# Staging of queries and keys split into four half buffers, with new scratch layouts in HBM

## The reference

```python
h = rmsnorm(x, norm1_g)
p = einsum('bsd,de->bse', h, w_in)          # u, then dq, dk, dv (4 heads x 2 x 64), then sq, sk, sv (4 heads x 64)
a_out = pool_mixer(u, pool_w, pool_scale)
b_out = diff_attention(dq, dk, dv, ...)     # softmax(q1 k1) - lam * softmax(q2 k2), causal, times v
c_out = stick_breaking_attention(sq, sk, sv, ...)
x = x + concat(a_out, b_out, c_out) @ w_out
x = x + (silu(rmsnorm(x) @ w_gate) * (rmsnorm(x) @ w_up)) @ w_down
return rmsnorm(x, final_norm_g)
```

## Time and profile before

| | us |
|---|---|
| median of 3 runs | 3868.71 (3867.44 to 3869.24) |
| the profiled execution | 3868.71 |
| its span, first to last instruction | 3867.0 |
| TensorE busy in it | 3738.0 |

### The profile page before, as it was taken

The page is one execution under the profiler, slowest core; times in us unless marked ns, Lnnn a source line. Parts: engine busy times, 40 slices in busy tenths (PEclk is TensorE's granted clock), DMA queues, the critical chain, the costliest instruction groups (busy, mean ns, idle before and its releaser), DMA issues.

```text
span 3867.0 us, 58782 instructions
## 1 busy us (share of the span) xinstructions
PE 3738.0 (97%) x24256; PEld 3121.5 (81%) x24256; DVE 1735.1 (45%) x3306; ACT 1424.1 (37%) x2568; POOL 485.5 (13%) x243
## 2 busy tenths in 40 slices
PE   8989999999999989899999999999999999999999
PEld 7878778978887878777788887788888777887887
DVE  5757624551644353444555444454445443122113
ACT  4322431331232343465555555444445541021001
POOL 2102130000000000233333301100000100000000
PEclk9999999999999999999999999999999999999999
DMA  8746677557655867666675754555554434564544
GB/s 307 263 164 232 231 265 258 200 207 252 217 192 191 290 201 259 213 222 235 230 248 206 242 202 146 170 170 169 166 166 169 156 131 161 195 235 163 196 185 163
DMA packets 198874, 799.34 MB, mean 207 GB/s; under 512 B 20816, under 2 KB 70224, under 8 KB 130384
## 3 DMA queue, kind: packets, MB, share of 16 engines
q1 hardware_dynamic: 198608, 795.59, 59.1%
HBM read 594.18 MB, written 201.33 MB: 206 GB/s over the span
## 4 chain that ended last, share of the span: by engine, by line
PE 89%; DVE 3%; ACT 3%; DMA 3%; issue 1%; POOL 0%; SPq 0%; DVEq 0%; ACTq 0%
PE bank L1365 85%; PE bank L1369 4%; DVE P L2433 1%; SPq L2625 0%; DMA zraw<-in_x_t_dram 0%; DMA R<-X1d 0%; POOL slot L2587 0%; DVE R L2104 0%; DMA Y2d<-PY 0%; DVE Z1a L2150 0%; ACT L1899 0%; DMA slot<-Wd 0%; ACT Z1a L1756 0%; DMA R<-in_x_n_dram 0%; ACT L1968 0%
## 5 line engine op out<-in xcount | busy, mean ns | idle before, releaser
L1365 PE MATMUL bank<-Z1a,slot 128*128 128x512 f32 x3048 | 782.1, 401 | 9.5 <-DVE slot L2045 9.5
L1365 PE MATMUL bank<-Z1b,slot 128*128 128x512 f32 x3048 | 782.6, 401 | 2.5 <-DVE Z1b L2150 2.5
L1365 PE MATMUL bank<-slot,Z0b 128*128 128x512 f32 (+1 forms) x3504 | 712.8, 354 | 9.9 <-DVE R L2104 8.8
L1365 PEld LDWEIGHTS bank<-Z1a,slot 128*128 128x128 f32 x3048 | 564.2, 189 | 139.8 <-DVE slot L2045 9.5
L1365 PEld LDWEIGHTS bank<-Z1b,slot 128*128 128x128 f32 x3048 | 566.3, 189 | 137.1 <-issue 7.0
L1365 PEld LDWEIGHTS bank<-slot,Z0b 128*128 128x128 f32 x3504 | 562.6, 189 | 104.3 <-DVE R L2104 11.6
L2587 POOL TENSOR_TENSOR slot<-raw,slot 128x1024 fp32r<-128x1024 f32 x117 | 292.1, 2503 | 688.9 <-ACT slot L1783 688.5
L2104 DVE TENSOR_TENSOR R<-R,bank 128x512 f32<-128x512 f32 x352 | 239.0, 686 | 244.6 <-PE bank L1365 244.3
L2599 POOL TENSOR_TENSOR Z0b<-AF,Z0b 128x512 fp32r<-128x512 f32 x88 | 142.0, 1614 | 1290.6 <-ACT Z0b L1975 1290.6
L2401 DVE TENSOR_SCALAR_CACHE_REDUCE P<-bank 128x512 f32<-128x512 f32 (+3 forms) x320 | 188.0, 609 | 255.1 <-PE bank L1365 254.2
L1365 PE MATMUL bank<-KS,DQ 128*128 128x512 f32 (+3 forms) x960 | 275.3, 388 | 21.6 <-DVE P L2401 9.4
(11 more groups left out here) (230 smaller groups left out, 4352.5 us busy)
## 6 DMA issues: line engine op xcount, KB each, us to landing
slot<-Wd SPq DMA_DIRECT2D x390, 1024.0 KB, 5.0
Wd<-slot SPq DMA_DIRECT2D x130, 1024.0 KB, 7.5
raw<-in_wts_dram SPq DMA_DIRECT2D x130, 512.0 KB, 4.3
DQ<-Qd SPq DMA_DIRECT2D x192, 128.0 KB, 3.7
DV<-Vd SPq DMA_DIRECT2D x60, 256.0 KB, 4.5
Kd<-QS SPq DMA_DIRECT2D x24, 512.0 KB, 5.1
Qd<-QS SPq DMA_DIRECT2D x24, 512.0 KB, 6.6
KS<-Kd SPq DMA_DIRECT2D x24, 512.0 KB, 7.1
```

What stands on the lines that cost most here:

```text
L1365: return e.matmul(o, a, b, start=start, stop=stop, skip_group_check=True)
```

## The change

`QS` becomes four buffers of 512 numbers per partition in the same space: two for high parts (0 and 2), two for low parts (1 and 3). High and low parts are stored by a transfer of their own each (256 KB): the high part waits for ScalarE only, the low part for VectorE. ScalarE now waits for the landing of the high part of two results ago, and for VectorE's reading of it; VectorE waits for the landing of the low part of two results ago. `Kd` becomes [head pair, high/low, partition, token], `Qd` becomes [head pair, 64, head of the pair, high/low, token], and `DQ` becomes [partition, 4, token]. The planner is not touched: the orders of TensorE, VectorE, ScalarE and GpSimd stay the same, and SyncE's gets 48 more issues (1298 rows where 1250 were).

```diff
-                  two("QS", [128, 2 * SUB]) + two("PT", [128, 16 + SUB]))
+                  two("QS", [128, SUB], F32, 4) + two("PT", [128, 16 + SUB]))
...
-        Kd = dram("Kd", [6, 128, 2, T])
-        Qd = dram("Qd", [6, T // 128, 128, 2, 128])
+        Kd = dram("Kd", [6, 2, 128, T])
+        Qd = dram("Qd", [6, 64, 2, 2, T])
...
-                mm(b[:, 0:w], DQ[:, qt, 2 * r, :], ks[:, at:at + w], True, False)
+                mm(b[:, 0:w], DQ[:, 2 * r, tok(qt)], ks[:, at:at + w], True, False)
...
-                i = m % 2
+                i = 2 * (m % 2)
                 if m >= 2:
                     act.wait_ge(*d_qs[i](*qkv_of[m - 2]))
                     if is_v(qkv_of[m - 2][2]):
                         act.wait_ge(*d_qv[i](*qkv_of[m - 2]))
+                    else:
+                        act.wait_ge(*dve_g("ev", ("C",) + qkv_of[m - 2][1:3]))
+                to = QS[i][:, :] if is_v(n) else QS[i][:, :].bitcast(F32R)
+                e.activation(to, b[:, :], ACT.Copy).then_inc(*act_g.inc("ev", label))
...
+                d = d_qs[i + 1]
+                if (k := qkv_of[m]) in d.at and d.at[k] > d.whole:
+                    dve.wait_ge(d.sem, d.at[k] - d.whole)
+                e.tensor_tensor(QS[i + 1][:, :].bitcast(F32R), b[:, :], QS[i][:, :], ALU.subtract).then_inc(
                     *dve_g.inc("ev", label))
...
-                sp.wait_ge(*dve_g("ev", ("C", s, n)))
-                if n % 2:
-                    to = Qd[x, NT * s:NT * s + NT].rearrange("c p a t -> p c (a t)")
-                    transfer(to, QS[i][:, :].rearrange("p (c n) -> p c n", c=NT), d_qs[i], *label)
-                else:
-                    to = Kd[x, :, :, SUB * s:SUB * s + SUB]
-                    transfer(to, QS[i][:, :].rearrange("p (a t) -> p a t", a=2), d_qs[i], *label)
+                t = slice(SUB * s, SUB * s + SUB)
+                for part in range(2):
+                    sp.wait_ge(*(dve_g if part else act_g)("ev", ("C", s, n)))
+                    to = Qd[x, :, :, part, t].rearrange("p h t -> h p t") if n % 2 else Kd[x, part, :, t]
+                    transfer(to, QS[i + part][:, :], d_qs[i + part], *label)
...
+                    at = SUB * s + 128 * x
                     for rep in range(2):
-                        to = DQ[64 * rep:64 * rep + 64, x, :, :].bitcast(F32).rearrange("p (h a) t -> p h (a t)", h=2)
-                        transfer(to, Qd[e_, NT * s + x].rearrange("(h p) a t -> p h (a t)", h=2), d_dq[x],
+                        to = DQ[64 * rep:64 * rep + 64, :, tok(x)].bitcast(F32)
+                        transfer(to, Qd[e_, :, :, :, at:at + 128].rearrange("p h a t -> p (h a) t"), d_dq[x],
                                  "ld", i, what, x)
```

More of the change, by code:

```diff
@@ L946, in build @@
         m = place([("R", [128, NT, D], F32)],
-                  two("QS", [128, 2 * SUB]) + two("PT", [128, 16 + SUB]))
+                  two("QS", [128, SUB], F32, 4) + two("PT", [128, 16 + SUB]))
         R = m["R"]
-        QS = [m[f"QS{i}"] for i in range(2)]
+        QS = [m[f"QS{i}"] for i in range(4)]
         PT = [m[f"PT{i}"] for i in range(2)]
@@ L963, in build @@
                      ("gb", [128, 2, D], F32), ("JK", [128, D], F32), ("DG", [128, SUB], F32)],
-                  two("KS", [128, 2048], F32R, 3) + [("DQ", [128, NT, 4, 128], F32R),
+                  two("KS", [128, 2048], F32R, 3) + [("DQ", [128, 4, SUB], F32R),
                    ("P0", [128, 2048], F32), ("P1", [128, 2056], F32), ("P2", [128, 2048], F32)] + two("TP", [128, SUB])
@@ L1022, in rows_of @@
             return x[SUB * s:SUB * s + SUB, :].rearrange("(c p) n -> p c n", p=128)
-        def parts_of(i, n):
-            if n % 2:
-                x = QS[i][:, :].rearrange("p (c a t) -> p c a t", c=NT, a=2)
-                return x[:, :, 0, :], x[:, :, 1, :]
-            return QS[i][:, 0:SUB], QS[i][:, SUB:2 * SUB]
         def heads_of(b):
@@ L1177, in build @@
         d_x1 = [landed(f"d_x1{c}", of("x1 out", lambda s, d, c=c: d == c)) for c in range(NT)]
-        d_qs = [landed(f"d_qs{i}", [qkv_of[m] for m in range(len(qkv)) if m % 2 == i]) for i in range(2)]
-        d_qv = [landed(f"d_qv{i}", [qkv_of[m] for m in range(len(qkv)) if m % 2 == i and is_v(qkv_of[m][2])]) for i in range(2)]
+        d_qs = [landed(f"d_qs{i}", [qkv_of[m] for m in range(len(qkv)) if m % 2 == i // 2 and (i % 2 == 0 or not is_v(qkv_of[m][2]))])
+                for i in range(4)]
+        d_qv = {i: landed(f"d_qv{i}", [qkv_of[m] for m in range(len(qkv)) if m % 2 == i // 2 and is_v(qkv_of[m][2])])
+                for i in (0, 2)}
         loads = of("ld")
@@ L1265, in staging_stored @@
         def staging_stored(e, s):
-            for i in range(2):
+            for i in range(4):
                 e.wait_ge(*d_qs[i](*[qkv_of[m] for m in sorted(qkv.values()) if qkv_of[m] in d_qs[i].at and qkv_of[m][1] == s][-1]))
+            for i in (0, 2):
                 e.wait_ge(*d_qv[i](*[qkv_of[m] for m in sorted(qkv.values()) if qkv_of[m] in d_qv[i].at and qkv_of[m][1] == s][-1]))
@@ L1557, in scores @@
                 pe.wait_ge(*d_dq[qt]("ld", i, "q", qt))
-                mm(b[:, 0:w], DQ[:, qt, 2 * r, :], ks[:, at:at + w], True, False)
+                mm(b[:, 0:w], DQ[:, 2 * r, tok(qt)], ks[:, at:at + w], True, False)
                 if c == len(ws) - 1:
                     mm(b[:, w - 128:w], ident_bf[:, :], mask_bf[:, 0 if e_ < 4 else 1, :], False, False)
-                mm(b[:, 0:w], DQ[:, qt, 2 * r + 1, :], ks[:, at:at + w], False, True).then_inc(*pe_sc.inc("sc", u, r, c))
+                mm(b[:, 0:w], DQ[:, 2 * r + 1, tok(qt)], ks[:, at:at + w], False, True).then_inc(*pe_sc.inc("sc", u, r, c))
             def transposes(u, g):
@@ L1741, in keys @@
                         act.wait_ge(*d_qv[i](*qkv_of[m - 2]))
-                if is_v(n):
-                    to, x = QS[i][:, 0:SUB], b[:, :]
-                else:
-                    to = parts_of(i, n)[0].bitcast(F32R)
-                    x = heads_of(b) if n % 2 else b[:, :]
-                e.activation(to, x, ACT.Copy).then_inc(*act_g.inc("ev", label))
+                    else:
+                        act.wait_ge(*dve_g("ev", ("C",) + qkv_of[m - 2][1:3]))
+                to = QS[i][:, :] if is_v(n) else QS[i][:, :].bitcast(F32R)
+                e.activation(to, b[:, :], ACT.Copy).then_inc(*act_g.inc("ev", label))
             def features(label, b):
@@ L2136, in keys @@
                 m = qkv["qkv out", label[1], label[2], 0]
-                hi, lo = parts_of(m % 2, label[2])
+                i = 2 * (m % 2)
                 dve.wait_ge(*act_g("ev", label))
-                e.tensor_tensor(lo.bitcast(F32R), heads_of(b) if label[2] % 2 else b[:, :], hi, ALU.subtract).then_inc(
+                d = d_qs[i + 1]
+                if (k := qkv_of[m]) in d.at and d.at[k] > d.whole:
+                    dve.wait_ge(d.sem, d.at[k] - d.whole)
+                e.tensor_tensor(QS[i + 1][:, :].bitcast(F32R), b[:, :], QS[i][:, :], ALU.subtract).then_inc(
                     *dve_g.inc("ev", label))
@@ L2700, in heads @@
                 label = ("qkv out", s, n, p)
-                i = qkv[label] % 2
+                i = 2 * (qkv[label] % 2)
                 if is_v(n):
                     x, t = {10: 0, 12: 2, 18: 4}[n], NT * s + 2 * p
-                    sv = QS[i][:, 0:SUB].rearrange("p (a n) -> p a n", a=2)
+                    sv = two_tiles(QS[i])
                     sp.wait_ge(*act_g("ev", ("C", s, n, p)))
@@ L2721, in stored @@
                     k = ("qkv out", z, n, p)
-                    sp.wait_ge(*(d_qv if part else d_qs)[qkv[k] % 2](*k))
+                    i = 2 * (qkv[k] % 2)
+                    if is_v(n):
+                        sp.wait_ge(*(d_qv if part else d_qs)[i](*k))
+                    else:
+                        for a in range(2):
+                            sp.wait_ge(*d_qs[i + a](*k))
             def attention_input(i, what, x):
@@ L2737, in attention_input @@
                         to = KS[m % 3][64 * part:64 * part + 64, 0:n].bitcast(F32)
-                        transfer(to, Kd[e_, 64 * x:64 * x + 64, part, 0:n], d, "ld", i, what, x)
+                        transfer(to, Kd[e_, part, 64 * x:64 * x + 64, 0:n], d, "ld", i, what, x)
                 elif what == "q":
```

2 lines of the change are left out of this document (removed).

## The result

| | before | after |
|---|---|---|
| median, us | 3868.07 (3866.7 to 3869.24, 4 runs) | 3971.37 (3970.74 to 3973.68, 4 runs) |
| ratio | | 1.0268, 95% interval 1.0250 to 1.0286 |
| span of the profiled execution, us | 3867.0 | 3969.4 |

What follows compares the result with a forecast made beforehand. TensorE was busy 3738.0 of 3867.0 us and DMA nearly used up in the projection windows; 252 us on two engines, less 94 free and 47 prefetched, gave 111, so 3868.7 + 111 = 3980 us, range 3888 to 4050.

Steps and rivals of the forecast that it cites:

- The narrow store is the term that decides: Query stores, outermost count 2: handed to two engines instead of 16, net 111 us on the path, bounds 70 to 158.
- The price, 12.0 us for a query tile on its engines: Query stores: each tile costs two engines 12.0 us instead of 1.5 on 16; 252 us over 24 tiles.
- Free time and prefetch, 94 and 47 us: Four projection windows: the two engines' free time (94 us) and prefetched weight loads (47 us) are subtracted from 252 us.
- the reserve of "three tiles": Weight prefetch: three tiles between a slot's load and use, 16.7 us, hide 11.7 us of delay once per window.
- A slower granted clock adds nothing: TensorE in the four windows: stalls may lower its clock, but slower matmuls hide while transfers set the pace; 0 us.
- The signs: Profile after: query store 8 us and more to landing, weight-load waits largest, QS waits for query stores, lower DMA share.
- ScalarE's and VectorE's waits run beside it: Staging buffers: ScalarE's new wait runs beside the two engines' delay; VectorE's bites when they are already late; nothing added.
- the split staging costs or gains nothing: Staging copies and subtractions, high half stored sooner: 0 us, since TensorE waits for neither; at best 6.7 us of key-load waits.
- SyncE's 48 more issues are free: SyncE's queue: 48 more transfers at 0.37 us each, 0 us on the path, 18 at the outside.
- Spread as before: Rival: query store still spread over 16 engines, 3868.7 us, under 7 gained or some 15 lost; chance 0.13.
- Hidden: Rival: two engines, but backlog drains between; only the first window overflows, 36 us or about 20, 3889 to 3905; chance 0.04.
- Early storing of the high half: Rival: keys reach attention sooner, both key-load waits (6.7 us) go, 3862; needs the spread store; chance 0.03.

Runs made afterwards that it cites:

- the two wide forms: Changed kernel with each query half stored over 16 engines: as two 64 x 512 transfers, one per head (1.0014), or as one 128 x 512 with Qd in rows (1.0008).
- 122 rows: Kernel with Qd in rows, storing each query half as 122 rows and then 6 rows: 3965.56 us, 1.0242 against the kernel before.
- The run on one engine: Kernel with Qd in rows, storing each query half as 127 rows and 1 row: +328 us, 1.0846 against the kernel before.
- The run on four engines: Kernel with Qd in rows, storing each query half as 124 rows and 4 rows: +33 us, 1.0076 against the kernel before.
- six buffers: Changed kernel with two staging buffers each for the low halves of keys and queries, store still 2 x 64 x 512: 3985.61 us, 1.0288.
- the two runs on ScalarE's queue: Changed kernel with its 2 x 64 x 512 query stores issued by ScalarE: 3957.07 us (1.0229); with six staging buffers too: 3950.66 us (1.0210).
- the high half alone: Kernel with Qd in rows, only the queries' high half stored as 122 and 6 rows, the low half as 64 and 64: +30 us, 1.0083.

## Why the prediction was right, and which of its parts were not

*The narrow store is the term that decides.* Right, and shown: by the two wide forms (1.0014, 1.0008), by the packet counts (2 small packets for each store on a queue of their own), and by 122 rows, which bring the loss back without any dimension of 2. The bet on two engines was the one place where no row could help.

*The price, 12.0 us for a query tile on its engines.* Somewhat too high. It comes from the mean rate of 21.8 KB per us; the query stores on a queue of their own took 10.6 (9.9 to 11.2). With 10.6 the first term would be (10.6 - 1.5) x 24 = 218 us, not 252, and the sum 218 - 94 - 47 = 77 us, not 111. The run on one engine came out under the account too, +328 against +399.

*Free time and prefetch, 94 and 47 us.* The sum came out near, 111 against 103, but its parts did not. By windows it said 36, 23, 27 and 25; the trace has 24, 8, 37 and 34. The step that failed is the reserve of "three tiles" put into every window alike, with the weight loads as the only ones that TensorE would wait for. In the first two windows TensorE works on projection tiles, waits for weights (6.0 and 5.7 us for `slot<-Wd`), and loses less than the account says. In the last two, attention stands between the tiles and the waits are for its loads: keys (11.5) and queries (6.7) in the third, values (19.7) in the fourth. That value load had no reserve at all: it was issued at 1560.33 us, when TensorE had been idle since 1555.2. The run on four engines shows the same split. The account gives nothing in any window there; TensorE's list shifts by 5, 0, 17 and 14 us in the four.

*A slower granted clock adds nothing.* Wrong as a statement about the account. TensorE's busy time rose by 20.6 us for the same matmuls, and the granted clock fell from 0.95, 0.99 and 0.96 to 0.91, 0.92 and 0.88 in the first, third and fourth window, in which TensorE stalled. These 20.6 us are a fifth of the difference. How much of them would have been waiting at full clock was not tried.

So the mechanism was foreseen, but that 111 lies so near to 103 is in part luck: a price and free time that err in opposite ways, and 82 us more idle time where 111 was forecast, filled up by 20.6 us of slower matmuls.

*The signs.* ScalarE's and VectorE's waits at QS and the lower DMA share came. Waits for weight loads as the largest entry did not: they are 11.9 us, less than values. The prediction also said that waits for DQ or KS would point to the 512 B runs or to late stores. They did appear (6.7 and 11.5 us), but the 512 B runs are not the cause: the wide forms have the same runs, and waits of at most 7.0 us for keys and 2.2 for queries.

*ScalarE's and VectorE's waits run beside it.* Right: six buffers took VectorE's 82.6 us away and gained nothing. But the sentence that the split staging costs or gains nothing holds for quick stores only; with slow ones the change gave 14 to 21 us back.

*SyncE's 48 more issues are free.* Right in the wide forms. In the changed kernel an issue itself can take long. The query loads' issues after (min/median/max in ns):

```profile
L2622 SPq DMA_DIRECT2D DQ<-Qd x192: 517/605/9562, 1285.0 to 3140.9; - x192
```

and before:

```profile
L2625 SPq DMA_DIRECT2D DQ<-Qd x192: 574/601/2029, 1245.4 to 3038.2; - x192
```

The longest went from 2.0 to 9.6 us. I read this as SyncE standing still at an issue until the two engines' rings have room, and with it all that is behind in its list; this reading is not tested by itself. In the two runs on ScalarE's queue the longest issue of a query load is 2.0 and 2.1 us, the late value load is gone, and most of the loss stays. So SyncE's issues are not free with narrow stores, but they carry some 20 us at most.

*The rivals.* "Spread as before" is out, since the packet count says two engines; the sign named for it, the query store's time to landing, could not be read. "Hidden" (3889 to 3905) is what four engines or the high half alone give, not this change. Early storing of the high half won no time in the wide forms: the keys' waits are 7.0 us in one and 4.3 in the other (6.7 before), and neither form is faster.

## What to carry to other kernels

Before a layout is changed, look at the outermost count of both sides of each transfer: here a "head" dimension of 2 in front put half a megabyte on 2 of 16 engines, and 24 such tiles cost 103 us. Price a hot spot by the busy time of the one engine that it lands on, not by the mean share; and do not subtract all of its free time: attention's loads have little reserve (one value load here went out after TensorE had begun to wait for it), and even a small burst was felt: 33 us for 108 on four engines. The layout that serves both the store and the load was one step away: rows of [high/low, partition], read as (high/low, head).

## What the runs showed that I had not expected

A store's engines can be read off the count of small packets: 16 for each wide transfer, 2 for each of 2 x 64 x 512, 2 + 6 for 122 and 6 rows. And moving the narrow stores to another queue left 81 us of the loss. Another queue took away SyncE's long issues; the loads on the old queue were late all the same.

A wait can change its name and stay: with six buffers the 19.7 us for a value load became 19.6 us of "issue" at the same matmul. The sum of waits for one releaser is not what would be won without it; the matmul's time is to be compared.
